# Retention heads: rotated queries and keys transposed in 32x32 blocks by VectorE and a round trip through DRAM instead of on TensorE

## The reference, cut to what matters

```python
q = (h @ wq).reshape(B, S, H, dk).transpose(0, 2, 1, 3).astype(jnp.float32)
k = (h @ wk).reshape(B, S, H, dk).transpose(0, 2, 1, 3).astype(jnp.float32)
...
q = rotary(q, pos)
k = rotary(k, pos) * (dk ** -0.5)
...
inner = jnp.einsum('bhid,bhjd->bhij', qi, ki) * decay_in
o = (jnp.einsum('bhij,bhje->bhie', inner, vi) + ...)
```

## Time and profile before

| | |
|---|---|
| median of 3 runs | 2500.69 us (2500.33 to 2501.09) |
| the profiled execution | 2501.11 us |
| its span in the trace | 2499.2 us |
| mean granted TensorE clock | 0.999 of full speed |
| busy: TensorE, VectorE, ScalarE, POOL | 2482.1, 1909.8, 1403.9, 136.3 us |
| DMA | 526.45 MB, mean 211 GB/s |
| retention stage | about 1090 to 1815 us of the span |

### The profile page before, as it was taken

How to read it: one execution, slowest core, us unless ns; L and a number is a source line. 1 busy time by engine, 2 the same in 40 slices (tenths; PEclk the granted TensorE clock), 3 DMA queues, 4 the chain that set the end, 5 groups by cost and what they waited for, 6 DMA issues and landing times. The chain is left out here.

```text
span 2499.2 us, 30109 instructions
## 1 busy us (share of the span) xinstructions
PE 2482.1 (99%) x11186; PEld 2055.6 (82%) x11186; DVE 1909.8 (76%) x2110; ACT 1403.9 (56%) x1697; POOL 136.3 (5%) x232
## 2 busy tenths in 40 slices
PE   9999999999999999999999999999999999999998
PEld 7888888888888888878888888888888888888887
DVE  6455556887988878987777877777988888788787
ACT  7454445655646556655566546555565555464564
POOL 0000000100100001100000000000001000010010
PEclk9999999999999999999999999999999999999999
DMA  8445456675756666755554655555767566667573
GB/s 311 156 161 176 144 193 222 217 250 179 273 181 239 232 227 219 253 195 185 189 201 167 232 188 180 178 184 206 244 242 247 196 242 221 217 230 241 189 282 137
DMA packets 146103, 526.45 MB, mean 211 GB/s; under 512 B 18096, under 2 KB 18352, under 8 KB 145072
## 3 DMA queue, kind: packets, MB, share of 16 engines
q1 hardware_dynamic: 131328, 476.65, 53.9%
q0 software_dynamic: 14496, 47.72, 6.1%
q10 hardware_dynamic: 144, 0.26, 0.0%
HBM read 502.55 MB, written 22.02 MB: 210 GB/s over the span
## 5 line engine op out<-in xcount | busy, mean ns | idle before, releaser
L1898 DVE TENSOR_TENSOR w_lo<-raw,w_hi 128x1024 fp32r<-128x1024 f32 x696 | 849.4, 1229 | 310.5 <-ACT w_hi L1325 307.0
L1325 ACT ACTIVATE w_hi<-raw 128x1024 fp32r<-128x1024 f32 x696 | 729.8, 1058 | 615.4 <-PE acc L888 216.4
L886 PE MATMUL acc<-w_hi,xT_hi 128*128 128x512 f32 x826 | 323.0, 391 | 2.8 <-DVE xT_lo L1963 1.5
L888 PE MATMUL acc<-w_hi,xT_lo 128*128 128x512 f32 x826 | 321.7, 389 | 0.0
L887 PE MATMUL acc<-w_lo,xT_hi 128*128 128x512 f32 x826 | 321.5, 389 | 0.0
L1325 ACT ACTIVATE w_hi<-scratch 128x1024 fp32r<-128x1024 f32 x201 | 211.8, 1057 | 169.3 <-PE acc L888 74.1
L1898 DVE TENSOR_TENSOR w_lo<-scratch,w_hi 128x1024 fp32r<-128x1024 f32 x201 | 244.3, 1218 | 67.7 <-ACT w_hi L1325 67.1
L886 PE MATMUL sc<-w_hi,xT_hi 128*128 128x512 f32 x736 | 287.7, 391 | 0.0
L888 PE MATMUL sc<-w_hi,xT_lo 128*128 128x512 f32 x736 | 286.7, 390 | 0.0
L887 PE MATMUL sc<-w_lo,xT_hi 128*128 128x512 f32 x736 | 286.5, 389 | 0.0
L886 PE MATMUL acc<-w_hi,aT_hi 128*128 128x512 f32 x600 | 233.8, 390 | 0.0
(11 more groups left out here) (275 smaller groups left out, 3913.4 us busy)
## 6 DMA issues: line engine op xcount, KB each, us to landing
raw<-in_w_stream SPq DMA_DIRECT2D x724, 512.0 KB, 4.4
scratch<-in_w_stream SPq DMA_DIRECT2D x171, 512.0 KB, 4.6
park<-stage POOLq DMA_DIRECT2D x38, 512.0 KB, 3.2
evac<-park POOLq DMA_DIRECT2D x152, 128.0 KB, 3.2
gain<-in_gains POOLq DMA_DIRECT2D x4, 1024.0 KB, 7.8
h<-in_x SPq DMA_DIRECT2D x2, 1024.0 KB, 8.7
scratch<-in_gn POOLq DMA_DIRECT2D x8, 256.0 KB, 4.4
scratch<-in_x_t SPq DMA_DIRECT2D x3, 512.0 KB, 8.3
```

The lines of the kernel that those rows point to most:

```text
L886: pe.matmul(bank[:, :], x_hi, w_hi[:, c], start=start, stop=False, skip_group_check=True)
L888: return pe.matmul(bank[:, :], x_lo, w_hi[:, c], start=False, stop=stop, skip_group_check=True)
L1325: act.activation(w_hi[:, slot * SW:(slot + 1) * SW], mlp_raw(u, load_of(u, t)), ACT.Copy).then_inc(mlp_hi, 1)
L1898: dve.tensor_tensor(w_lo[:, c], mlp_raw(u, load_of(u, t)), w_hi[:, c].bitcast(F32), ALU.subtract).then_inc(mlp_lo, 1)
```

## The change

The eight transposes of a head leave TensorE. When both tokens are rotated, VectorE transposes the 32x32 blocks of `stage` into `evac`, behind `lo` of tile 7 (`turn_qk_blocks`). POOL's queue writes `evac` to a new DRAM tensor and reads it back in four DMAs into `qkT` (`turn_qk`). ScalarE puts the pieces into order with one copy of 128x1024 into the scratch space of the rotation (`queries_and_keys`), behind `hi` of tile 16, in place of the two copies out of PSUM. TensorE's scores stand behind tile 12 instead of tile 9 and wait for that copy. VectorE's `decayed` stands behind `lo` of tile 18 instead of 15. `scaled_o` has one more wait, for the write to DRAM, since it writes `evac`. The counts of what was staged for TensorE change with it.

```diff
--- before.py
+++ after.py
@@ -238,7 +239,7 @@
 
     staged, of_turn = QUADS, []
     ups = SUPER * QUADS
-    for quads, turns in ((ups, ups), (QUADS, OF_FOUR), (2 * RET_HEADS, 0), (QUADS, OF_FOUR), (ups, ups)):
+    for quads, turns in ((ups, ups), (QUADS, OF_FOUR), (RET_HEADS, 0), (QUADS, OF_FOUR), (ups, ups)):
         of_turn += [staged + q + 1 for q in range(turns)]
         staged += quads
     return of_turn
@@ -379,6 +380,8 @@
         decay_t = cut(3456, 384)
         gn_t = cut(3840, RET_V)
         rot = cut(4352, 4 * S)
+        ret_qkT = rot
+        qk_tiles = qkT.rearrange("p (a t j r) -> p t j a r", a=GRID, t=TOKS, j=NB // P)
 
 
         y = raw
@@ -427,6 +430,8 @@
         acc_done = pair("acc_done")
         acc_out = pair("acc_out")
         staged = pair("staged")
+        rotated_made, qk_turned, qk_parked, qk_fetched, qk_made = (
+            sem(name) for name in ("rotated_made", "qk_turned", "qk_parked", "qk_fetched", "qk_made"))
         tr_done = pair("tr_done")
         tr_hi = pair("tr_hi")
         tr_out = pair("tr_out")
@@ -483,6 +488,7 @@
         turned, parked, fetched = sem("turned"), sem("parked"), sem("fetched")
         turn_hi_made, turn_out = sem("turn_hi_made"), sem("turn_out")
         park = nc.dram_tensor("park", (TURNS, P, TOKS * NB), F32, kind="Internal").ap()
+        qk_park = nc.dram_tensor("qk_park", (RET_HEADS, P, TOKS * NB), F32, kind="Internal").ap()
 
         block = ctx.enter_context(nc.Block())
 
@@ -597,7 +603,7 @@
 
             fox_staged = QUADS
             mlp_staged = SUPER * QUADS + QUADS
-            ret_staged = RET_HEADS * 2 + QUADS
+            ret_staged = RET_HEADS + QUADS
             last_use = [0, fox_staged, fox_staged + mlp_staged, fox_staged + mlp_staged + ret_staged]
 
             def load_gain(n):
@@ -624,11 +630,23 @@
                 turn(n)
             pool.wait_ge(mlp_lo, MLP_TILES)
 
+            def turn_qk(hd):
+
+                pool.wait_ge(qk_turned, hd + 1)
+                pool.dma_start(qk_park[hd], evac_both[:, :]).then_inc(qk_parked, 16)
+                pool.wait_ge(qk_parked, 16 * (hd + 1))
+                wait(pool, score_done, FOX_HEADS + hd)
+                rows = qk_park[hd].rearrange("(a c) (b k) -> b c a k", a=GRID, b=GRID)
+                for g in range(GRID):
+                    pool.dma_start(qkT[g * TB:(g + 1) * TB, :].rearrange("p (a k) -> p a k", a=GRID),
+                                   rows[g]).then_inc(qk_fetched, 16)
+
             def head(hd):
                 wait(pool, inner_made, hd)
                 wait(pool, gated[1], hd)
                 pool.dma_start(decay_t, decay[hd]).then_inc(table_in, 16)
                 pool.dma_start(gn_t, gn[hd]).then_inc(table_in, 16)
+                turn_qk(hd)
                 pool.wait_ge(table_in, hd * 32 + 32)
                 for t in range(TOKS):
                     pool.wait_ge(silu_made[t], hd + 1)
@@ -1029,8 +1047,8 @@
 
                 for t in range(TOKS):
                     pe.wait_ge(tr_out[t], T(f"tr{t}"))
-                q = [qkT[:, dd * S:(dd + 1) * S] for dd in range(2)]
-                k = [qkT[:, (2 + dd) * S:(3 + dd) * S] for dd in range(2)]
+                pe.wait_ge(qk_made, hd + 1)
+                q, k = ([ret_qkT[:, (part + dd) * S:(part + dd + 1) * S] for dd in range(2)] for part in (0, 2))
                 for dd in range(2):
                     pe.matmul(tr[0][:, 0:S], k[dd][:, 0:P], q[dd], start=(dd == 0), stop=(dd == 1))
                 for dd in range(2):
@@ -1072,11 +1090,7 @@
             def value_gate_pair(hd):
 
                 def between(t):
-                    if t == TAU2:
-                        own()
-                    if t == TAU4:
-                        pending()
-                    if t == SEVEN + 2:
+                    if t == SEVEN + 5:
                         ret_scores(hd)
                     if t == SEVEN + REST + 2:
                         ret_mix(hd)
@@ -1421,6 +1435,7 @@
 
             def scaled_o(hd):
                 act.wait_ge(grstd_made, hd + 1)
+                act.wait_ge(qk_parked, 16 * (hd + 1))
                 for t in range(TOKS):
                     act.activation(evac[t][:, :], mix[t][:, :], ACT.Copy, scale=factor(t, grstd)).then_inc(o_out, 1)
 
@@ -1530,6 +1545,12 @@
                 seven_pair(u, "up" if i % 4 < 2 else "down", was, i % 2 * 2, (i - 1) % 2 * 2, new_sums=new_sums,
                            turn=turn_of_pair(m, i), own_turn=UPS_AT[m] + i // 4 * QUADS + i % 4 * 2)
 
+            def queries_and_keys(hd):
+
+                act.wait_ge(qk_fetched, GRID * 16 * (hd + 1))
+                act.activation(ret_qkT.rearrange("p (j t a r) -> p t j a r", j=NB // P, t=TOKS, a=GRID),
+                               qk_tiles, ACT.Copy).then_inc(qk_made, 1)
+
             def query_key_block(hd):
 
                 u = head_unit(hd)
@@ -1601,13 +1622,11 @@
                     s_high(a_sums, False, ret_sums)
                 hi(u, 8)
                 hi(u, 9)
-                hi(u, 10)
-                batch_qk(0, qkT)
-                hi(u, 11)
-                hi(u, 12)
-                batch_qk(1, qkT)
-                for t in range(13, 19):
+                for t in range(10, 17):
                     hi(u, t)
+                queries_and_keys(hd)
+                hi(u, 17)
+                hi(u, 18)
 
             def wo_pair(half, n):
 
@@ -2182,8 +2201,6 @@
                            normed=m == 0 and i >= PAIRS - 2, new_sums=new_sums, end=m == 1 and i == PAIRS - 1,
                            turn=turn_of_pair(m, i), own_turn=UPS_AT[m] + i // 4 * QUADS + i % 4 * 2)
 
-            staged_by_mlp = QUADS + SUPER * QUADS + QUADS
-
             def rotated(hd, tok):
 
                 dve.wait_ge(qk_out[tok], hd + 1)
@@ -2197,7 +2214,13 @@
                 dve.tensor_tensor(r[2], e[:, :, 0, :], sin, ALU.mult)
                 step(dve.tensor_tensor(r[3], e[:, :, 1, :], cos, ALU.mult))
                 dve.tensor_tensor(o[:, :, 0, :], r[0], r[1], ALU.subtract)
-                dve.tensor_tensor(o[:, :, 1, :], r[2], r[3], ALU.add).then_inc(staged[tok], 1)
+                dve.tensor_tensor(o[:, :, 1, :], r[2], r[3], ALU.add).then_inc(rotated_made, 1)
+
+            def turn_qk_blocks(hd):
+
+                dve.wait_ge(rotated_made, TOKS * (hd + 1))
+                dve.transpose(evac_both[:, :].rearrange("p (b m r) -> p m b r", b=GRID, r=TB),
+                              stage_both[:, :].rearrange("p (m b c) -> p m b c", b=GRID, c=TB)).then_inc(qk_turned, 1)
 
             def decayed(hd):
 
@@ -2281,9 +2304,10 @@
                 lo(u, B22)
                 rotated(hd, 0)
                 lo(u, TAU4)
-                dve.wait_ge(staged[0], staged_by_mlp + 2 * hd + 1)
+                dve.wait_ge(rotated_made, TOKS * hd + 1)
                 rotated(hd, 1)
                 lo(u, 7)
+                turn_qk_blocks(hd)
                 if new_sums:
                     s_low(A_SUMS_OF_RET + hd // RET_HALF, False, ret_sums)
                 lo(u, 8)
@@ -2294,11 +2318,9 @@
                 v_part(u, ret_parts)
                 lo(u, 12)
                 g_part(u, ret_parts)
-                for t in range(13, 16):
+                for t in range(13, 19):
                     lo(u, t)
                 decayed(hd)
-                for t in range(16, 19):
-                    lo(u, t)
 
             def wo_pair(half, n):
 
```

## The result

The changed kernel takes 2513.15 us (median of 6 runs, 2507.88 to 2516.01) against 2500.54 us of the kernel before (6 runs, 2500.16 to 2501.09): ratio 1.0046, 95% interval 1.0036 to 1.0056. It is slower by 12.6 us; I had forecast 2495.0 us.

The account below looks back on a forecast made before the run. The prediction took TensorE's issued work as the bound. Its terms, -7.5 + 0.9 + 0.8 = -5.8 us, gave 2495.3 or 2494.9, stated as 2495.0 us; range 2492.8 to 2501.5, the forecast's own 2493.5 to 2496.9.

Parts of the forecast that it names:

- Part 1: TensorE in the heads' value and gate pairs: removing two transpose batches per head, 0.47 us each, saves 7.5 us.
- Part 2: VectorE's added transpose behind tile 7: only tile 8 in heads 1 and 5 comes late, +0.9 us in all.
- Part 3: The way through DRAM to ScalarE's copy: wait per head between nothing and 2.1 us, taken as +0.8 us in all.
- the term +0.8 us: TensorE's waits for the copy at the scores: 0.1 us each put for heads that miss by a little.
- copy late, slower: Rival: ScalarE's copy held behind a load delayed by the turn's traffic; 2506.1 us, at the bound 2510.9; chance 0.12.
- -7.5: Time saved on TensorE by dropping 16 transpose batches of 0.47 us in eight heads, in us.
- +0.9: Tile 8 in heads 1 and 5, late by 0.36 us, 0.47 with the restart: cost over two heads, in us.

Follow-up runs that it names:

- run 4: Changed kernel with ScalarE's copy reading VectorE's blocks directly, DRAM write and fetches left out: 2495.11 us, ratio 0.9978 to the kernel before.
- run 1: Changed kernel with ScalarE's copy of queries and keys behind tile 14's high part instead of tile 16's: 2499.97 us, ratio 0.9995 to the kernel before.
- run 2: Changed kernel with TensorE's scores behind tile 13 instead of 12, the copy unmoved: 2498.69 us, ratio 0.9990 to the kernel before.
- run 3: Changed kernel with ScalarE's copy reading VectorE's blocks directly, DRAM write and fetches still running: 2509.88 us, ratio 1.0043 to the kernel before.
- Runs 10 and 11: Changed kernel with copy, scores and mostly the mix moved; the second also puts VectorE's transpose behind tile 8 in heads 1 and 5: 2493.29 and 2492.36 us.

## Why the prediction was wrong, point by point

- **Part 1 held.** The head without a wait is 0.93 us shorter (0.94 forecast), TensorE has 64 transposes less, and without traffic the stage gains what was worked out (5.6 us from mix to mix).
- **Part 2 held.** VectorE's transpose takes 1.24 us, and tile 8 is late in heads 1 and 5 alone: 0.45 us lost each against 0.47. Its last sentence, that the low parts of v cost nothing at the mix, holds in the changed kernel, where the waits at the scores come first, and without traffic (run 4). With the traffic and without those waits, runs 1 and 2 show it at 4.4 and 3.1 us in four heads.
- **Part 3 failed, at the term +0.8 us.** Measured, that term is 14.3 us of lateness at the scores and 6.3 of the clock behind it, 20.6. "The load lands near 1272.4 and the copy ends at 1274.5, just in time" rests on a landing time of 4.3 us, at worst 6.4. Measured in head 1: 8.4 for tile 16's load, 9.3 and 9.2 for the two before it. Two inputs were too kind. I priced the added bytes at the loads' rate, 3.5 us per head; they take 4 to 5. And I let free share absorb 1.8 us of it and halved what was left. The chain can't do that: each load is issued when a slot comes free, three in-order tiles stand ahead of the copy, and each was late. (The halving does not give 1272.4 exactly either: 1269.9 + 1.16 + 0.85 is 1271.9; this changes nothing.) My price of the fetches themselves, 3.2 us each, was also short (7.8 in head 1): from the issue of the write to the last landing it was 14.4 us in head 1 and 13.7 in head 2, where I had 8.6. In the changed kernel this is hidden behind tile 16, as run 3 shows; run 1 lays it bare. The Trainium skill, DMA: Bandwidth & Descriptors, Queues, rings and completion order, says that each DMA engine takes turns between the queues for which it has work; a load beside fetches from POOL's queue would then get only part of each engine. The loads' 8.8 us against 4.8 fit that; no run here shows the turns themselves, and they would not tell why the rate as a whole fell from 299 to 250 GB/s, which stays open.
- **The example.** I worked the copy through head 2, which turned out to be the only head whose copy was in time. Counted from the first mix of the head before, since every head here starts late, I had the copy end at 1274.5 - 1215.93 = 58.6 us, at worst 60.6. In head 2 it was 58.4, so there the forecast came out, but by luck: the second profile of the same kernel has 60.3 in head 2 and a wait, and in this one heads 1, 3 and 5 have 62.1, 61.4 and 61.4, beyond my upper bound, and heads 6 and 7 60.6 and 60.2. Heads 1, 3 and 5 lose 2.2 to 2.9 us at the scores, against at most 2.1.
- **What no part had:** the clock. After the three longest waits, 2.07 to 2.78 us, TensorE ran at 1.2 GHz and lost 6.3 us more. That is why the result lies above even the end of the rival that came true, "copy late, slower" at 0.12 (up to 2510.9): waits at the scores of 13.3 + 1.0 (head 0) and the clock's 6.3 are 20.6; with -7.5 and +0.9 this gives +14.0, against 14.9 between the profiled executions. Without the clock's 6.3 it would be +7.7, inside that rival's +5.4 to +10.2.
- **The rule against the change.** By the Trainium skill, VectorE: DVE Perf Modes, Rules for kernel authors, the transposes belonged on TensorE. For the kernel as changed the trace agrees, by 12.6 us. Runs 10 and 11 disagree: with the consumers moved, the transposes are better off TensorE, ratios 0.9968 and 0.9967, with 5.5 to 5.9 us of the gain shown from mix to mix. Which is better is set here by whether the detour's traffic makes a consumer late, not by the transpose itself.

## What to carry to other kernels

In this kernel, work moved off the bounding engine paid its full length only where every in-order queue that its result passes kept its slack; so put a detour's consumer by the landing times with the detour's own traffic in flight, not by those of the trace before. When a copy is placed behind another load's work in an in-order queue, it inherits that load's lateness. And a sum worked through one head of eight says little of the others, where landing times differ by microseconds from head to head. And where a fix moves one consumer later, move its successors with it: here the scores alone gave 0.9990, scores, copy and mix together 0.9968.

## What was unexpected of the hardware

- Four fetches of 128 KB beside the weights' loads nearly doubled the loads' time to land (4.8 to 8.8 us) at the same busy share of the DMA engines, while the rate fell from 299 to 250 GB/s. In the stretch 1193 to 1201 us it was 4.8 before, 8.4 with the full bytes, and with a quarter of them 6.1 in four transfers or 6.4 in one.
- 4 KB rows instead of 1 KB pieces hardly changed that (8.3 us, and the same number of packets on the page).
- TensorE's granted clock fell to 0.50 after idle times of 2.07, 2.55 and 2.78 us at the scores, and not after 0.88 to 1.85; each of these falls cost 1.7 to 2.9 us. Over all traces the lengths overlap: it also fell after 1.89 and 1.95 us (the changed kernel, two profiles), and did not after 1.97 (run 2, 1098.8 us) and 2.27 (run 3).
- A DMA queue's share of the engines' time moved from 6.1% to 6.4% at the same 47.72 MB (before, run 4), so a price for a MB from two pages is good to a fifth or so.
